# A hybrid decoder block on one core: the first norm's scale row by a broadcast transfer, and ten filler products at the start of TensorE

## The reference, cut to what matters

```python
h = x * rsqrt(mean(x * x, axis=-1) + 1e-6) * norm_mix      # x: (512, 1024), norm_mix: (1024,)
proj = h @ w_in            # w_in: (1024, 4648): q, k, v of two attentions, indexer, two gates
# stick-breaking attention, 8 heads of 64; sparse attention with a top-128 indexer, 8 heads over 2 KV heads
x = x + (sigmoid(g_sb) * (o_sb @ w_branch_sb) + sigmoid(g_sa) * (o_sa @ w_branch_sa)) @ w_out
x = x + square(relu(rmsnorm(x, norm_mlp) @ w_ff1)) @ w_ff2   # inner width 4096
```

## Time and profile before

| | |
|---|---|
| median of three runs | 726.17 us (725.69 to 727.34) |
| span of the profiled execution | 724.9 us |
| what lies around the span | 1.27 us, if the median is put beside it; the profiled execution's own time is shown only as its span |
| TensorE busy | 716.9 us, 99% of the span |
| VectorE, ScalarE, GpSimd busy | 537.2, 341.9 and 259.6 us |
| all DMA queues | 70.65 MB, mean 97 GB/s |

### The profile page before, as it was taken

One profiled execution on the slowest core, in us unless ns is written; L12 is line 12 of the kernel. 1 busy time (PEld: TensorE's weight loads), 2 busy tenths in 40 slices (PEclk: granted clock), 3 DMA queues, 4 the chain that ended last, 5 costly groups with the idle time before them and its releaser, 6 DMA issues.

```text
span 724.9 us, 9771 instructions
## 1 busy us (share of the span) xinstructions
PE 716.9 (99%) x3454; PEld 575.0 (79%) x3454; DVE 537.2 (74%) x771; ACT 341.9 (47%) x492; POOL 259.6 (36%) x207
## 2 busy tenths in 40 slices
PE   8999999999999899999999999999999999999998
PEld 5878878787776666788888988888888888888887
DVE  7354889899886875537646569695968869595898
ACT  6244753365567777722324353624335253624441
POOL 2104325001223564003301080725427090725677
PEclk9999999999999999999999999999999999999999
DMA  9308231311110212133190235141330605131103
GB/s 331 142 15 252 97 115 60 117 59 59 59 59 23 51 45 59 59 117 117 32 345 1 65 110 175 59 168 64 114 118 17 213 1 174 58 116 58 59 1 117
DMA packets 44039, 70.65 MB, mean 97 GB/s; under 512 B 2657, under 2 KB 27489, under 8 KB 44002
## 3 DMA queue, kind: packets, MB, share of 16 engines
q1 hardware_dynamic: 44000, 70.16, 29.6%
q10 hardware_dynamic: 2, 0.00, 0.0%
HBM read 65.71 MB, written 2.10 MB: 94 GB/s over the span
## 4 chain that ended last, share of the span: by engine, by line
PE 94%; DVE 2%; POOL 1%; ACT 1%; issue 1%; DMA 0%; DVEq 0%; ACTq 0%
PE ps L1950 8%; PE ps L1951 8%; PE ps L1952 8%; PE ps L1979 7%; PE ps L1980 7%; PE ps L1981 7%; PE ps L436 6%; PE ps L438 6%; PE ps L437 6%; PE ps L429 6%; PE ps L431 6%; PE ps L430 6%; PE ps L1861 1%; PE ps L1755 1%; PE ps L1871 1%; PE ps L1789 1%
## 5 line engine op out<-in xcount | busy, mean ns | idle before, releaser
L1950 PE MATMUL ps<-b_hi,cut_hi 128*128 128x512 f32 (+1 forms) x280 | 104.1, 372 | 0.0
L1951 PE MATMUL ps<-b_lo,cut_hi 128*128 128x512 f32 (+1 forms) x280 | 103.8, 371 | 0.0
L1952 PE MATMUL ps<-b_hi,cut_lo 128*128 128x512 f32 (+1 forms) x280 | 103.8, 371 | 0.0
L653 POOL TENSOR_TENSOR a_lo<-qo_sb,a_hi 128x512 fp32r<-128x512 f32 x56 | 91.8, 1666 | 14.2 <-ACT a_hi L976 14.2
L436 PE MATMUL ps<-cut_hi,a_hi 128*128 128x512 f32 x216 | 86.4, 400 | 0.0
L438 PE MATMUL ps<-cut_hi,a_lo 128*128 128x512 f32 x216 | 84.5, 391 | 0.0
L437 PE MATMUL ps<-cut_lo,a_hi 128*128 128x512 f32 x216 | 84.3, 390 | 0.0
L965 ACT ACTIVATE qo_sb<-ps 128x512 f32<-128x512 f32 x32 | 19.2, 599 | 130.3 <-PE ps L1952 86.3
L420 DVE TENSOR_TENSOR cut_lo<-raw,cut_hi 128x2048 fp32r<-128x2048 f32 (+2 forms) x33 | 51.2, 1551 | 27.5 <-ACT cut_hi L412 27.4
L661 POOL TENSOR_TENSOR qo_sb<-qo_sb 128x512 f32<-128x512 f32 x7 | 9.1, 1295 | 154.0 <-DVE qo_sb L1409 154.0
L412 ACT ACTIVATE cut_hi<-raw 128x2048 fp32r<-128x2048 f32 (+2 forms) x33 | 48.5, 1470 | 31.1 <-PE ps L431 22.7
(11 more groups left out here) (218 smaller groups left out, 1652.3 us busy)
## 6 DMA issues: line engine op xcount, KB each, us to landing
raw<-in_w_ff_dram SPq DMA_DIRECT2D x32, 1024.0 KB, 5.5
raw<-in_w_in_dram SPq DMA_DIRECT2D x16, 1024.0 KB, 5.8
gates<-in_x_dram SPq DMA_DIRECT2D x8, 512.0 KB, 5.5
raw<-in_w_out_dram SPq DMA_DIRECT2D x4, 1024.0 KB, 5.1
raw<-in_w_in_dram SPq DMA_DIRECT2D x4, 512.0 KB, 6.9
raw<-in_w_branch_sb_dram SPq DMA_DIRECT2D x2, 1024.0 KB, 5.1
raw<-in_w_branch_sa_dram SPq DMA_DIRECT2D x4, 512.0 KB, 6.9
out_dram<-gates SPq DMA_DIRECT2D x7, 256.0 KB, 2.1
```

What stands on the lines that cost most here:

```text
L1950: T.matmul(dst, w_hi[:, w], b_hi[:, k, a:b], start=(k == 0), stop=False)
L1951: T.matmul(dst, w_hi[:, w], b_lo[:, k, a:b], start=False, stop=False)
L1952: mm = T.matmul(dst, w_lo[:, w], b_hi[:, k, a:b], start=False, stop=(k == KD - 1))
```

## The change

`norm_mix` is no longer loaded as one row and multiplied out by TensorE. SyncE issues one transfer behind x tile 0 that writes the row to all 128 partitions of a free part of `gates` (`slot(12, 2)`, 512 KB written), and VectorE waits for that one transfer and reads the scale row from there instead of from PSUM. The row of ones, its memset, ScalarE's row load and TensorE's two products go. `WARM` becomes (10, 0): ten fillers stand ahead of the first transposes, where one stood, and none in the middle of `first_tile`, where two stood.

```diff
-WARM = (1, 2)
+WARM = (10, 0)
...
-        mix_row = lg[0:1, 1, 0:D]
+        mix_gain = slot(12, 2)
...
-        one_row = dist[0:1, 0:P]
...
             sp.dma_start(x_tok[:, 0, :], x_d[0:P, :]).then_inc(x_in[0], 16)
+            sp.dma_start(mix_gain, norm_mix.to_broadcast([P, D])).then_inc(mix_gain_in, 16)
...
-            pool.memset(one_row, 1.0).then_inc(one_row_made, 1)
...
-            act.dma_start(mix_row, norm_mix).then_inc(mix_row_in, 16)
...
-            mix_gain = ps[:, 6 * S:8 * S]
+            dve.wait_ge(mix_gain_in, 16)
             for hf in range(2):
                 w = slice(hf * S, (hf + 1) * S)
-                dve.wait_ge(mix_spread, hf + 1)
                 norm_scale(0, x_tok[:, 0, w], x_tok[:, 0, w], mix_gain[:, w])
...
-            pe.wait_ge(one_row_made, 1)
-            pe.wait_ge(mix_row_in, 16)
-            for hf in range(2):
-                T.matmul(bank(6 + hf), one_row, mix_row[:, hf * S:(hf + 1) * S], start=True, stop=True).then_inc(mix_spread, 1)
             pe.wait_ge(const_cut, 1)
             keep_warm(WARM[0])
```

## The result

The changed kernel took 726.89 us (median of 13 runs, 726.53 to 728.72), the kernel before 725.69 us (13 runs, 725.37 to 727.34): ratio 1.0017, with a 95% interval of 1.0009 to 1.0024. It is 1.2 us slower. I had forecast 0.1 us less. Two later comparisons of the same two kernels, on two chips, gave 1.0019 (1.0010 to 1.0028) and 1.0025 (1.0015 to 1.0035).

What follows compares the result with a forecast made beforehand. TensorE, busy 716.9 of 724.9 us, was taken as the bound. With -0.14 us for an early clock rise and +0.1 for the rise as before, it took -0.1 from the median 726.17: 726.0 us, range 724.9 to 727.4.

Steps and rivals of the forecast that it cites:

- The marker: Start of the projection's next tile on TensorE, 17.82 us in the first profile; moving it was to move the kernel's end.
- TensorE's rise: TensorE's change from half speed (1.2 GHz) to full speed (2.4 GHz), read at 13.3 us in the first profile.
- The marker becomes 9.73 + 7.95 = 17.68, against 17.82: At the kernel's start: x tile 1 landing 2.3 us later plus the work behind it puts the marker 0.14 us earlier.
- 7.95 us from x tile 1 on: Chain from x tile 1's landing through squares, high and low parts and 14 matmuls to the marker: 7.95 us.
- case A: Rival: broadcast as fast as a plain transfer (1.4 us) and an early clock; marker 16.8, 725.1 us; chance 0.19.
- the 1.27 us around the span: The median time before lay 1.27 us above the profiled span of 724.9 us.
- What they can give is the clock: Ten fillers ahead of the transposes, 4.3 us and hidden, could bring TensorE's full speed some 6 us forward.
- so it gives nothing: An early clock gains nothing with loads 2.3 us late, as transposes and ten matmuls wait for VectorE anyway.
- B (3.3 us): Rival: the broadcast takes 3.3 us, x tile 1 lands at 10.7, marker 18.7, 727.1 us; chance 0.18.
- Case C: Rival: TensorE's idle gaps behind the fillers keep the clock down to 16.4 us; marker 19.4, 727.7 us; chance 0.15.

Runs made afterwards that it cites:

- experiments 10 and 7: 10: the kernel before, unchanged, profiled once more, span 724.7 us. 7: the kernel before without the two fillers in its first tile, 726.71 us, ratio 0.9999.
- experiment 11: The changed kernel, unchanged, for one more profiled execution; the marker at 17.66 us, no time or ratio given.
- experiment 1: The kernel before, run again unchanged: ratio to itself 0.9995, spans 723.4 to 725.1 us.
- experiments 13 to 15: Same rounds: changed kernel unchanged, 727.74 us; with seven fillers behind the first transposes and two in the tile, 726.54; with a 4 KB row load replacing the broadcast, 726.38.

## Why the prediction was wrong

**What held.** The broadcast takes some 2.3 us of the queue: the row landed at 6.47 (forecast 6.5), the half slab at 8.0 (7.9), x tile 1 at 9.5 (9.7); the last two are 2.4 and 2.1 later than before. The scaling started at 6.48 (6.6), the fillers were hidden, and no load was waited for behind 18 us. The marker of the changed kernel is 17.82, in the stated 17.6 to 17.9, with 17.66 in it and 17.99 and 17.95 just above it in three more profiles (forecast 17.68). The bound of the loads, measured with the clock held, is 17.5 and 17.7.

**The step that failed** is the other side of the difference: "The marker becomes 9.73 + 7.95 = 17.68, against 17.82". I took 17.82 as the kernel before. It was the slowest of four draws of TensorE's rise. The four markers of before have a mean of 17.07, the four of the changed kernel 17.86. That is 0.8 of the 1.2 us, at the lower end of the interval (0.65 to 1.7 us). The rest may lie in the ends, which come long or short. How often each kernel has the long end stays open, so I can't split the 1.2 us to the end.

My own rows had what was needed: 7.95 us from x tile 1 on, applied to the kernel before with tile 1 at 7.43, gives 15.4 as the loads' bound; with the low part of slab 0 at 13.27 and 3.26 behind it, VectorE's bound is 16.5 (measured: 16.54 and 16.40 in experiments 10 and 7, and 16.11 where fast transposes brought ScalarE's and VectorE's work forward). The profiled kernel before stood 1.3 above its bound only through the clock, the changed one 0.3 above its own. An execution with an earlier rise gains up to 1.3 us before, and 0.3 after. I named this in case A for one direction and did not draw it for the forecast.

All 17 profiles bear this out. In the seven in which the clock was up for good by 10 us, and in that of experiment 11, the marker is 8.03 to 8.08 us behind the start of ScalarE's squares of tile 1, near my 7.95. In the other nine, with a rise near 11.5 to 14, it is 8.3 to 9.2 behind. The squares start at 8.40 to 8.58 in the four profiles of before, and at 9.50 to 9.67 in the four of the changed kernel. With the clock up this puts the bounds at 16.4 to 16.7 and at 17.5 to 17.8. Between the bounds the late loads cost 1.1 us, where my sum had a gain of 0.14. My table had a sign of it, the 1.27 us around the span; the runs show 1.7, so that the profiled execution was some 0.9 us slower than the median of 13.

**The fillers.** "What they can give is the clock": they did in three of four profiles, but the gap behind them lost it again near 10 us. That they wait for VectorE, "so it gives nothing", was too small: with the transfer alone the time is 1.1 us higher, and the marker 0.7 to 1.0 later. My sum had the slow clock end at 13.3 in every case; without ten fillers it ended near 14.0, and two fillers stood on the path.

**The rivals.** Case A (fast loads) and B (3.3 us) fell with the landing at 6.5. Case C named the gaps, and the clock does fall there. But it had them keep the clock down until 16.4, and the clock was back by 13.6 in every profile of the changed kernel, so its price was wrong. The Trainium skill (TensorE: Matmul & The Clock Gate, part 1) says that idleness brings the half rate back, and the windows of the changed kernel agree: 0.50 from 10 us on, behind 0.26 us busy of 1.00. The figures of the Trainium skill for large transfers (DMA: Bandwidth & Descriptors, Bandwidth), 341 GB/s at 1 MB and 425 at 16 MB, are not reached under the broadcast of 512 KB: from 4.0 to 5.5 us the queue moved 147 to 238 GB/s.

**The scope of a difference.** 1.2 us is 0.17%. It is within the 0.2% that I had called no change, and yet 13 runs told it from nothing.

## What to carry to other kernels

One profile is one draw: where an engine's clock rises at a different time in each execution, compute the bound that remains with the clock up, for both kernels, and compare bounds before comparing profiles. A 512 KB transfer put ahead of others on a full queue delays all of them by its length (2.1 to 2.4 us here), and the broadcast from one row took longer than a plain transfer of the same size (2.3 against 1.4 us). Fillers can bring the clock early, but in the three profiles where they had, the 2 us of little work behind them gave it back; with seven more fillers there it stayed up in two profiles of two.

## What the runs showed of the hardware that I had not expected

The end of the span comes in two lengths. In the kernel before, the nine output transfers landed in 1.7 to 2.2 us in two of four profiles, and in up to 3.7 or 3.8 in the other two. The rows of the output tensor in the changed kernel (short end) and in experiment 1 (long end), issue time min/median/max in ns, and us to landing:

```profile
L551 SPq DMA_DIRECT2D out_dram<-gates x9: 332/333/361, 717.2 to 722.9; - x9
DMA to landing us min/median/max: 1.8/2.1/2.3
```

```profile
L553 SPq DMA_DIRECT2D out_dram<-gates x9: 332/431/1542, 716.2 to 721.9; - x9
DMA to landing us min/median/max: 2.1/2.8/3.7
```

In the long one an issue takes 1.54 us, and the span ends 1.1 us later behind the same last matmul. The profiles with ten fillers ahead of the transposes had the short end 7 times in 8, those with one filler there 2 times in 9. But all profiles of the changed kernel come from its lower group of spans (experiments 13 to 15), so this count doesn't tell how its other executions ended.

The traces hold one thing that goes with it in all 17 profiles: a transfer of 0.02 MB on the queue that the profile calls `instruction`. The queue in the changed kernel from 711 to 713 us (short end), and in experiment 1 from 718 to 720.5 us (long end):

```profile
q8 instruction: 1, 0.02, 3.0%
```

```profile
q1 hardware_dynamic: 364, 0.65, 70.9%
q8 instruction: 1, 0.02, 3.0%
```

In the nine profiles with the short end the last such transfer starts at 710.0 to 712.0 us, ahead of the first output transfer. In the eight with the long end it starts at 718.1 to 720.4, among the output transfers and beside the issue that takes 1.54 to 1.71 us. So a load of instructions may be what lengthens the end; no run moves it on purpose, and what sets its time is open. In my profiles the end doesn't carry the loss: before had the long one twice in four and the changed kernel never, and their spans differ by only 0.4 us in the mean. In the times it may.

The granted clock reads 1.00 from the start of the trace to the first recorded fall, also where matmuls of 512 columns start 0.43 us apart, the spacing of 1.2 GHz. Only after a fall, as in the changed kernel, does that column show the 0.50.
